# The low parts of a weight panel in four GpSimd instructions of 512 columns

## The reference

```
u = rmsnorm(h); z = u @ w_in                      # block 1: pool, q, k, v and gate columns
y = gates * (pool_mixer(p) @ w_pool, moba_attention(q, k, v) @ w_attn)
h = h + rmsnorm(m @ w_out)
a = square(relu(rmsnorm(h) @ w_up)); h = h + rmsnorm(a @ w_down)
shift, scale, gate = split(silu(c) @ w_ada + b)   # block 2: modulation from c
h = rmsnorm(x) * (1 + scale) + shift
... depthwise convolution of 31 taps, SSM scan of 32 heads, gates, w_out
x = x + gate * ((silu(g) * up) @ w_ffn_down); out = rmsnorm(x)
```

## Time and profile before

| | us |
|---|---|
| median of 3 runs | 1905.27 |
| lowest, highest | 1903.21, 1905.36 |
| the profiled execution | 1902.58 |
| its span | 1900.8 |
| TensorE busy in it | 1776.7 (93%) |
| VectorE busy | 994.5 (52%) |
| GpSimd busy | 707.5 (37%) |
| ScalarE busy | 654.1 (34%) |

### The profile page before, as it was taken

One profiled execution on the slowest core, in us unless ns is written; L12 is line 12 of the kernel. 1 busy time (PEld: TensorE's weight loads), 2 busy tenths in 40 slices (PEclk: granted clock), 3 DMA queues, 4 the chain that ended last, 5 costly groups with the idle time before them and its releaser, 6 DMA issues.

```text
span 1900.8 us, 21685 instructions
## 1 busy us (share of the span) xinstructions
PE 1776.7 (93%) x7970; PEld 1428.6 (75%) x7970; DVE 994.5 (52%) x1378; ACT 654.1 (34%) x804; POOL 707.5 (37%) x169
## 2 busy tenths in 40 slices
PE   7999999898999999569999999988999999999997
PEld 5667776677878787458787877867888778888886
DVE  4444366483535355579879787886436431101112
ACT  4332253421212122324443434447332332222231
POOL 3233332524344444323232323422344334464443
PEclk9999999899999999689999999999999989999999
DMA  4111212244444434112222222221222312242232
GB/s 167 67 67 66 88 46 87 89 159 140 158 152 143 166 134 142 45 68 89 108 92 89 90 98 99 88 89 45 89 89 88 111 67 100 100 152 90 101 113 96
DMA packets 30198, 193.25 MB, mean 102 GB/s; under 512 B 3360, under 2 KB 3360, under 8 KB 11328
## 3 DMA queue, kind: packets, MB, share of 16 engines
q1 hardware_dynamic: 23184, 158.89, 23.6%
q10 hardware_dynamic: 6960, 33.62, 5.2%
HBM read 190.34 MB, written 2.16 MB: 101 GB/s over the span
## 4 chain that ended last, share of the span: by engine, by line
PE 74%; DVE 18%; issue 4%; ACT 2%; POOL 0%; DVEq 0%; ACTq 0%; DMA 0%; SPq 0%; POOLq 0%
PE gemm_bank L424 17%; PE gemm_bank L425 17%; PE gemm_bank L431 17%; PE gemm_bank L478 6%; PE gemm_bank L462 5%; PE gemm_bank L471 3%; DVE arena L1496 3%; PE gemm_bank L466 3%; DVE arena L1507 2%; DVE aux_bank L1597 2%; DVE arena L1411 1%; DVE arena L1492 1%; PE aux_bank L545 1%; DVE scratch L1660 1%; PE aux_bank L502 1%
## 5 line engine op out<-in xcount | busy, mean ns | idle before, releaser
L400 POOL TENSOR_TENSOR w_lo<-w_raw,w_hi 128x2048 fp32r<-128x2048 f32 x147 | 687.1, 4675 | 1164.0 <-ACT w_hi L897 1164.0
L424 PE MATMUL gemm_bank<-a_hi,w_hi 128*128 128x512 f32 x1224 | 491.1, 401 | 2.7 <-DVEq L1614 2.4
L425 PE MATMUL gemm_bank<-a_lo,w_hi 128*128 128x512 f32 x1224 | 480.7, 393 | 0.0
L897 ACT ACTIVATE w_hi<-w_raw 128x2048 fp32r<-128x2048 f32 x147 | 280.3, 1907 | 226.2 <-PE gemm_bank L431 173.0
L431 PE MATMUL gemm_bank<-a_hi,w_lo 128*128 128x512 f32 x1224 | 308.8, 394 | 2.5 <-POOL w_lo L400 2.5
L424 PEld LDWEIGHTS gemm_bank<-a_hi,w_hi 128*128 128x128 f32 x1224 | 231.8, 189 | 59.6 <-issue 12.4
L431 PEld LDWEIGHTS gemm_bank<-a_hi,w_lo 128*128 128x128 f32 x1224 | 228.5, 188 | 54.3 <-issue 4.0
L425 PEld LDWEIGHTS gemm_bank<-a_lo,w_hi 128*128 128x128 f32 x1224 | 232.0, 190 | 48.3 <-issue 1.9
L1597 DVE SCALAR_TENSOR_TENSOR aux_bank<-scratch,gcol,aux_bank 128x511 f32<-128x511 f32 (+14 forms) x240 | 167.8, 733 | 14.5 <-ACT aux_bank L1089 11.9
L462 PE MATMUL gemm_bank<-a_hi,w_hi 128*128 128x512 f32 x352 | 132.1, 421 | 25.1 <-ACT a_hi L907 16.7
L424 PE MATMUL gemm_bank<-b_hi,w_hi 128*128 128x512 f32 x368 | 146.0, 397 | 0.0
(11 more groups left out here) (264 smaller groups left out, 2213.8 us busy)
## 6 DMA issues: line engine op xcount, KB each, us to landing
w_raw<-weights_dram SPq DMA_DIRECT2D x147, 1024.0 KB, 4.8
arena<-ada_dram ACTq DMA_DIRECT2D x32, 768.0 KB, 4.2
acc<-cum_rows ACTq DMA_DIRECT2D x8, 512.0 KB, 3.9
row_b<-cum_rows ACTq DMA_DIRECT2D x8, 512.0 KB, 4.2
h<-x_t_dram SPq DMA_DIRECT2D x4, 512.0 KB, 7.5
out_t_dram<-arena SPq DMA_DIRECT2D x8, 256.0 KB, 2.2
cols<-cols_dram SPq DMA_DIRECT2D x1, 279.0 KB, 2.9
poolw<-pool_w_dram SPq DMA_DIRECT2D x1, 256.0 KB, 11.0
```

The source lines that it names most:

```text
L400: pool.tensor_tensor(wlo[s][:, :], raw[s][:, :], whi[s][:, :].bitcast(F32), ALU.subtract) \
L424: pe.matmul(gemm_bank[bank][:, :], whi[slot][:, w], hi[:, k, :], start=(n == 0), stop=False)
L425: pe.matmul(gemm_bank[bank][:, :], whi[slot][:, w], lo[:, k, :], start=False, stop=False)
L897: act.activation(whi[panel % 2][:, :], raw[panel % 2][:, :], ACT.Copy).then_inc(w_hi_ready, 1)
```

## The change

GpSimd's instruction of 2048 columns becomes four instructions of 512 columns, one behind the other, over the same operands. Only the last of the four raises w_lo_ready; only the first stands behind the two waits. On every other engine the instructions and their order are the same as before. GpSimd's queue holds 588 such instructions in place of 147.

```diff
@@
 MASKED = 1e33
+LOW_PIECES = 4
@@
             def low_parts(i, s):
                 pool.wait_ge(w_loaded[s], 16 * i + 16)
                 pool.wait_ge(w_hi_ready, 2 * i + s + 1)
-                pool.tensor_tensor(wlo[s][:, :], raw[s][:, :], whi[s][:, :].bitcast(F32), ALU.subtract) \
-                    .then_inc(w_lo_ready, 1)
+                for q in range(LOW_PIECES):
+                    w = slice(q * PANEL // LOW_PIECES, (q + 1) * PANEL // LOW_PIECES)
+                    ins = pool.tensor_tensor(wlo[s][:, w], raw[s][:, w], whi[s][:, w].bitcast(F32), ALU.subtract)
+                    if q == LOW_PIECES - 1:
+                        ins.then_inc(w_lo_ready, 1)
```

## The result

The kernel with four pieces takes **1861.47 us**, the median of 4 runs (1860.34 to 1862.51), against 1905.30 for the kernel before (4 runs, 1903.21 to 1905.36). The ratio is 0.9768 with a 95% interval of 0.9755 to 0.9782. The profiled span fell from 1900.8 to 1860.8 us, by 40.0, where the sum of the prediction said 39.6. Lines of the file have moved by 3 or 4: L400 is now L403, L462, L471 and L478 are L466, L475 and L482, and so on.

The account below looks back on a forecast made before the run. GpSimd's long subtractions hold up VectorE, for which TensorE waits. Terms 15.2 + 4.4 + 8.3 + 3.2 + 6 + 1.5 + 1 = 39.6 us off 1902.6 gave 1863.0, plus 2.7 for the median: 1866 us, range 1852 to 1905.

Parts of the forecast that it names:

- The price of a piece: GpSimd's panels: a piece of 512 columns takes 1.12 to 1.15 us, 1.47 at the far end.
- the way in: Between two GpSimd pieces: VectorE goes first and the next piece begins after it, with no semaphore between them.
- Rival (a): VectorE gets in between pieces, but a piece costs 1.3 to 1.47 us: 1883 to 1898 us; chance 0.12.
- Rival (b): Port never free between pieces, VectorE still waits for the whole panel: 1905 us, no change; chance 0.10.
- rival c: VectorE shut out for the whole panel and each piece pays its start, 0.13 us: 1915, up to 1939; chance 0.13.
- the pace of group 1: MLP of block 1: VectorE wins 1.3 us per panel, 3.9 per group; 15.2 us over four groups.
- the clock in groups 2 to 4: MLP: TensorE's slow matmuls behind b_hi waits go, three of four penalties at 1.5 us each, 4.4 us.
- TensorE's new wait for w_lo: MLP group 1: grows from 1.2 to some 4 us, hidden since VectorE sets the end of that group.
- Attention: Four waits of TensorE for the last L1411 of a head go entirely, 8.3 us, plus a clock term of 3.2.
- the clock term of the third and fourth iteration: Attention: the slower iterations at a granted clock of 0.83 behind the L1411 wait go, 3.2 us.
- SSM, squares, dt: SSM groups win 6 us (bounds 0 and 9.9), the L1779 wait 1.5, the dt chain 1 of 11.4.
- Start, FFN, loads: Start of the kernel, FFN and loads of panels: nothing won or lost, counted 0.

Follow-up runs that it names:

- p2: Two pieces of 1024 columns in place of the changed kernel's four: 1885.11 us, ratio 0.9907 to the kernel before.
- p8: Eight pieces of 256 columns in place of the changed kernel's four: 1866.95 us, ratio 0.9811 to the kernel before.
- half: Changed kernel with each panel's even blocks computed first and a second semaphore for them, still four pieces: 1861.95 us, ratio 0.9765.
- mlp_one: Changed kernel with one piece per panel in GpSimd's second loop (MLP of block 1, dt panel), four in the others: 1884.94 us, ratio 0.9901.
- bound: Changed kernel, but after the first two panels GpSimd computes only 128 of a panel's 2048 columns, in one instruction: 1823.66 us, ratio 0.9563.
- late: Changed kernel, but GpSimd starts the third panel of the dt stage only when VectorE has finished cum: 1862.83 us, ratio 0.9766.
- mix: Changed kernel with eight pieces in GpSimd's third loop (dt stage, SSM, gates, FFN), four in the first two: 1861.92 us, ratio 0.9768.
- half_late: Changed kernel with even blocks first, a second semaphore, and the third dt panel held back until cum is there: 1859.62 us, ratio 0.9752.

## Why the prediction was right

**The price of a piece and the way in (terms, rivals a, b).** Held. In alternation L1500, L1503 and L1511 were longer by 0.3, 0.9 and 1.0 us (walked through: 0.2, 1.0, 1.1). The pass ends 7.33 us after L1511 (496.26 to 503.59), for 7.3, and the period of two tiles is 10.4 us, as written. Rival (a) fell with that. VectorE gets in between two pieces although no semaphore stands between them. Rival (b) fell, and with it the reading of the Trainium skill, "GPSIMD Engine Reference", section "Instruction dispatch": that a core may start the next instruction as soon as its share of the last is done may be so, but this trace has VectorE between the two each time (7.90 us for pieces that take 5.03 alone). The Trainium skill, "SBUF — State Buffer", section "Who interferes with whom", has the shared ports as an exclusive lock held for an instruction; the trace agrees, and p2 and p8 show the hold going with the instruction's size (at most 2.26 and 0.59 us).

**The start of a piece (rival c).** Its price was right (5.03 - 4.61 = 0.42 us for three more starts, 0.14 each; 0.13 was written), its consequence not: it needed VectorE to be shut out as in (b). The pass of 5.03 us stays below the 5.2 that were named as the limit, and no one waits for it where it runs alone.

**MLP.** 17.0 us instead of 19.6, the largest miss. Two terms were mis-sized: the pace of group 1, and the clock in groups 2 to 4. In group 1 the claim that TensorE's new wait for w_lo is hidden because VectorE sets the end was true for TensorE and not for VectorE: TensorE came so late and at half clock that L1496 twice waited for it (0.69 and 0.51 us), and VectorE's work on the group, from the copy L1349 to the last L1511, was 1.4 us shorter instead of 3.9. In half, without that wait, it was 3.9 us shorter, and so was the group (94.9 to 91.0), just the term of the sum with the one clock penalty that it kept. The wait that I called hidden cost 0.9 us; TensorE idles as long in both, and is busy for 79.2 us instead of 78.1.

In groups 2 to 4 the waits went entirely: TensorE's idle time fell from 12.5 to 0.4 us, where the pace terms were 11.3. Its busy time fell by only 1.9 us (277.2 to 275.3), where the clock term was 4.4. That term took the lower clock for a price of the b_hi wait alone. In the changed kernel it comes in each of these groups behind 24 matmuls of one column (L652), with no wait in front of them. TensorE's timeline in the first of these groups, and the stretch by engine right behind it:

```profile
441.41 2.73 PE L652 MATMUL aux_bank<-ones,arena 128*128 128x1 f32 x24
```

```profile
444.40:447.80 3.40, 3.40 (x10) 2.62 (x9) 0.00 (x0) 0.00 (x0) 3.40 (x4) 0.50 0.00 0
```

The same follows at 536.6 and 628.7; in the kernel before only one of these three places has it (557.7), in mlp_one two (449.6 and 644.2), and these lie in the groups at 0.95. What remains against bound's 272.6 is clock (0.98 against 0.99), not a wait.

**Attention.** 12.1 us up to the branches against 11.5, and 0.9 in the branches and the merge, counted 0. The wait of 8.3 and the clock term of the third and fourth iteration went as written: the iterations are now 58.0 us apart each, where the earlier trace rows had 60.2 and 61.8, and the granted clock is 1.00 where the earlier trace rows had 0.83. The chain that ended last, in the changed kernel:

```profile
78.47 3.87 PE gemm_bank L466 x16
...
136.46 3.85 PE gemm_bank L466 x16
...
194.41 3.85 PE gemm_bank L466 x16
```

**SSM, squares, dt.** 6.3, 1.5 and 1.5 us, for 6, 1.5 and 1. The waits for L1685 (9.9 us) are 4.2 now; L1664 (L1660 in the earlier trace rows, 3.25 us) takes 0.92 in the mean, and the three subtractions of L1783 take 0.86 and, for two, 3.25. In dt two panels take 12.40 us where the earlier trace rows had 9.62. The dt term was small for the right reason: late, mix, half and half_late moved the pieces about, and none brought TensorE's next matmul more than 1.5 us nearer to the end of the MLP.

**Start, FFN, loads.** 0.7 us in all, for 0.

**The sum.** The MLP fell short by 2.6 us and the rest brought 3.0 more, so that 40.0 stand against 39.6. That the total is so close is partly luck: the clock term of the MLP was 2.5 us too large, other stages made up for it, and the clock alone moves the whole by 3 to 5 us. The forecast of 1866 added 2.7 us to the sum's 1863.0, since the profiled execution of before lay that far below its median. After, the profiled execution (1862.51) was the slowest of its four, so the median came out at 1861.47; those 2.7 us were scatter, and belonged into the range.

## What to carry to other kernels

Where two engines exclude each other for the length of an instruction, cut the instruction of the engine that nobody waits for to about the size of the other's instructions, here 1.1 us beside 0.7; half that number of pieces won 3.7 of 17.0 us in the MLP, twice the number won nothing more. Price it by what the held engine sets (a period, a chain), and ask of the longer pass not only whether its consumer waits, but whether the engine behind the consumer does. Where the work has to cross a saturated chain, moving it from one wait to the next brought little here; less of it would bring more (bound, 38 us).

## What was not expected of the hardware

- VectorE gets in after each GpSimd instruction, with no semaphore between them: over all 1378 of its instructions the longest hold is one piece. Small instructions are held too: copies of 32 and 98 columns 1.1 and 0.8 us in late. Eight pieces of 256 columns still leave VectorE 84 us above its time without them (909.7 against 825.6).
- The waits of about 4 us before w_lo and b_hi were followed by the lower of TensorE's two clocks (1.2 GHz, granted clock 0.57 to 0.59 in stretches of 4 us) wherever they stood, and 16 matmuls then take 5.27 instead of 3.63 us. Moving such a wait moved this price with it. The lower clock also came with no wait at all, behind 24 matmuls of one column (0.50 in 444.40 to 447.80), in some groups and not in others.
- The granted clock differs between kernels with the same waits: 95.2 to 96.2 us for an MLP group at 0.98, 97.9 to 98.5 at 0.95, and 578.0 to 583.1 us for a last stage in which the waits differ by less than 1 us. It is enough to keep the parts of a change from adding up to better than some 5 us here.
